# A two-block transformer on one core: eight-column norm sums, whole splits ahead of the residual, one norm for two, and a lone first weight block

## What is computed

```python
x = x + 0.5 * swiglu(rmsnorm(x, ffn1_norm_g), ffn1_w_in, ffn1_w_out)        # phase 0
x = x + merged @ w_mix_out                                                   # phase 1 (mix1)
x = x + 0.5 * swiglu(rmsnorm(x, ffn2_norm_g), ffn2_w_in, ffn2_w_out)        # phase 2
x = rmsnorm(x, final_norm_g)                                                 # phase 3 (final)
for i in range(2):          # phases 4, 5 (mix2), 6 and 7, 8 (mix3), 9
    h = modulate(rmsnorm_2(x, norm_g[i, 0]), sh1, sc1)     # h * (1 + scale) + shift
    x = x + 0.5 * g1 * swiglu_2(h, ffn_w13[i, 0], ffn_w2[i, 0])
    h = modulate(rmsnorm_2(x, norm_g[i, 1]), sh2, sc2)
    x = x + g2 * mixer(h)                                  # i == 0: pool and SSD; i == 1: attention
    h = modulate(rmsnorm_2(x, norm_g[i, 2]), sh3, sc3)
    x = x + 0.5 * g3 * swiglu_2(h, ffn_w13[i, 1], ffn_w2[i, 1])
return rmsnorm_2(x, final_norm_g_2)                                          # phase 10 (final)
```

## Time and profile before

| | before |
|---|---|
| median of 3 runs | 1699.43 us (1697.11 to 1700.32) |
| the profiled execution | 1698.5 us |
| its span, first to last instruction | 1696.7 us |
| PE busy | 1662.9 us (98%) |
| DVE busy | 1202.4 us (71%) |
| ACT busy | 809.9 us (48%) |
| mean granted PE clock | 0.996 |

### The profile page before, as it was taken

How to read it: one execution, slowest core, us unless ns; L and a number is a source line. 1 busy time by engine, 2 the same in 40 slices (tenths; PEclk the granted TensorE clock), 3 DMA queues, 4 the chain that set the end, 5 groups by cost and what they waited for, 6 DMA issues and landing times.

```text
span 1696.7 us, 34452 instructions
## 1 busy us (share of the span) xinstructions
PE 1662.9 (98%) x14542; PEld 1627.7 (96%) x14542; DVE 1202.4 (71%) x1303; ACT 809.9 (48%) x874; POOL 87.1 (5%) x110
## 2 busy tenths in 40 slices
PE   9999999999999999999998899999999999999998
PEld 9999999999999999999997899999999987899998
DVE  5888876676788887888867688756545566765444
ACT  5444456654544444444565553445444456554442
POOL 0000000000000000000004000000000003200000
PEclk9999999999999999999999999999999999999999
DMA  7988744344498875988533359653654443335551
GB/s 311 346 331 312 279 174 174 125 166 158 146 354 318 303 276 187 340 312 320 205 141 125 125 201 345 247 188 135 224 197 175 174 148 125 125 141 208 198 189 59
DMA packets 50491, 365.08 MB, mean 215 GB/s; under 512 B 5728, under 2 KB 5856, under 8 KB 6240
## 3 DMA queue, kind: packets, MB, share of 16 engines
q1 hardware_dynamic: 39744, 287.04, 46.0%
q0 software_dynamic: 10368, 75.50, 12.0%
q10 hardware_dynamic: 288, 1.18, 0.2%
HBM read 362.65 MB, written 1.05 MB: 214 GB/s over the span
## 4 chain that ended last, share of the span: by engine, by line
PE 88%; DVE 7%; ACT 3%; issue 1%; DMA 0%; SPq 0%; ACTq 0%; DVEq 0%
PE bank L252 50%; PE bank L284 24%; PE bank L267 3%; PE bank L244 3%; DVE wlo L184 2%; PE bank L357 2%; PE bank L1662 1%; PE bank L369 1%; DVE m_p L1427 0%; DVE m_e L1924 0%; ACT whi L176 0%; DVE x L309 0%; ACT m_e L1803 0%; DVE x L401 0%; PE bank L1231 0%
## 5 line engine op out<-in xcount | busy, mean ns | idle before, releaser
L184 DVE TENSOR_TENSOR wlo<-raw,whi 128x2048 fp32r<-128x2048 f32 x261 | 598.1, 2294 | 203.0 <-ACT whi L176 202.2
L252 PE MATMUL bank<-xh,whi 128*128 128x256 f32 x2608 | 728.0, 279 | 3.4 <-ACT gate L533 2.0
L252 PE MATMUL bank<-xl,whi 128*128 128x256 f32 x2608 | 723.3, 277 | 0.0
L252 PE MATMUL bank<-xh,wlo 128*128 128x256 f32 x2608 | 723.0, 277 | 0.0
L176 ACT ACTIVATE whi<-raw 128x2048 fp32r<-128x2048 f32 x261 | 498.4, 1913 | 312.5 <-PE bank L252 190.9
L252 PEld LDWEIGHTS bank<-xh,whi 128*128 128x128 f32 x2608 | 492.1, 189 | 6.1 <-issue 2.6
L252 PEld LDWEIGHTS bank<-xl,whi 128*128 128x128 f32 x2608 | 490.7, 188 | 0.1
L252 PEld LDWEIGHTS bank<-xh,wlo 128*128 128x128 f32 x2608 | 490.7, 188 | 0.0
L284 PE MATMUL bank<-hid_hi,whi 128*128 128x256 f32 x1056 | 292.8, 277 | 0.0
L284 PE MATMUL bank<-hid_lo,whi 128*128 128x256 f32 x1056 | 291.9, 276 | 0.0
L284 PE MATMUL bank<-hid_hi,wlo 128*128 128x256 f32 x1056 | 291.9, 276 | 0.0
(11 more groups left out here) (317 smaller groups left out, 1822.7 us busy)
## 6 DMA issues: line engine op xcount, KB each, us to landing
raw<-stream_in SPq DMA_DIRECT2D x270, 1024.0 KB, 4.8
mod_raw<-mod_in POOLq DMA_DIRECT2D x72, 1024.0 KB, 7.0
params<-params_in SPq DMA_DIRECT2D x1, 1474.0 KB, 16.1
x<-x_in SPq DMA_DIRECT2D x2, 512.0 KB, 4.3
m_gsu<-sgu_in ACTq DMA_DIRECT2D x1, 1024.0 KB, 5.1
y_out<-x SPq DMA_DIRECT2D x1, 1024.0 KB, 3.8
consts<-consts_in SPq DMA_DIRECT2D x1, 280.5 KB, 4.8
tab_pos<-pos_in ACTq DMA_DIRECT2D x1, 128.0 KB, 3.5
```

The costliest lines, as they stand in the source:

```text
L184: dve.tensor_tensor(wlo[:, s, :], raw[:, s, :], whi[:, s, :].bitcast(F32), ALU.subtract)\
L252: last = pe.matmul(out[:, m, :], (whi, wlo)[wp][:, s, k * 256 + m * P:k * 256 + m * P + P], (xh, xl)[ap][:, k, :], start=(k == 0 and j == ...
```

## The change

- **Norm sums (`pe_norm`, `act_norm`).** DVE's pair sums are gone, but for phase 0; PE sums each of the eight tiles, 16 matmuls of one column where there were eight. The dummy matmuls between the sums are gone; 8 stand behind the sums (before: 14) and 20 behind the spread (before: 26).
- **The second block of the next phase** is split whole, and ahead of the residual: on ACT where the halves were, on DVE before `mod_store` and the residual. In phase 0 the halves stay, both ahead of the reciprocal.
- **The final norm inside (phase 3).** Phase 3 has no program of its own left. At the norm of phase 4 ACT also squares `x * g_final` tile by tile, PE sums both kinds, and DVE and ACT make both reciprocal roots at once. `dve_final_inside` writes `x` normed by the final norm within phase 4, behind the last group of `mod_sum`; PE's `mod_fold` waits for it.
- **Shift in the rounding.** Mixers 2 and 3 take the shift as ACT's bias like the FFNs. `xm` stays without it, and its rows get two more columns that hold the shift, so that the float32 products have the shift's part in a column of their own, which ACT adds as a bias.
- **The start.** SP waits for `x` after the first weight block, and then issues the second and third. DVE's pair sums of phase 0 stand ahead of the constants' copies.
- `gres` (the residual's gain) and `gmod` (the next norm's) are now made behind `xl`.

```diff
+W = T + 2
...
-        xm = sb("xm", [P, KD, T])
+        xm_wide = sb("xm", [P, KD, W])
+        xm = xm_wide[:, :, 0:T]
...
+            ni = norm_index[n]
+            act.activation(std[:, 8:9], cols[:, 64:65], ACT.Sqrt)
             for b in range(4):
                 if n == 0:
                     act.wait_ge(sem(f"x_loaded{b // 2}"), 16)
                 else:
-                    act.wait_ge(sem("x_updated"), 4 * (n - 1) + b + 1)
+                    act.wait_ge(sem("x_updated"), 4 * last_stage(n) + b + 1)
                 act.activation(xm[:, 2 * b:2 * b + 2, :], x[:, 2 * b:2 * b + 2, :], ACT.Square, scale=D ** -0.5)\
                    .then_inc(sem("x_squared"), 1)
+                if n == AFTER_FINAL:
+                    for k in (2 * b, 2 * b + 1):
+                        act.activation(final_squares[:, k, :], x[:, k, :], ACT.Square, scale=prm("g_final")[:, k:k + 1])\
+                           .then_inc(sem("final_step"), 1)
...
+                act_split_halves(act)
+            if n == AFTER_FINAL:
+                act.wait_ge(sem("final_step"), KD + 2)
+                act.activation(std[:, 0:4], std[:, 0:4], ACT.Sqrt, scale=1.0 / D).then_inc(sem("std_ready"), 1)
+            else:
+                act.wait_ge(sem("x_summed"), ni + 1)
+                act.activation(std[:, 0:2], STAT[:, T:T + 2], ACT.Sqrt, bias=cols[:, 64:65]).then_inc(sem("std_ready"), 1)
...
-        WARM = (14, 8, 14, 26)
+        WARM = (8, 20)
...
+            def column_sums(squares, k, c0, first, last):
+                for tt in range(2):
+                    mm = pe.matmul(STAT[:, c0 + tt:c0 + tt + 1], squares[:, k, tt * P:tt * P + P], ones[:, 0:1],
+                                   start=(first and tt == 0), stop=last, skip_group_check=True)
+                return mm
...
             for b in range(4):
...
-                if b >= 2:
-                    pe_keep_warm(pe, n, WARM[b - 2])
-                pe.wait_ge(sem("x_paired"), 4 * n + b + 1)
-                for tt in range(2):
-                    mm = pe.matmul(STAT[:, T + tt:T + tt + 1], xm[:, 2 * b, tt * P:tt * P + P], ones[:, 0:1],
-                                   start=(b == 0 and tt == 0), stop=(b == 3), skip_group_check=True)
+                if n == 0:
+                    pe.wait_ge(sem("x_paired"), b + 1)
+                    mm = column_sums(xm, 2 * b, T, b == 0, b == 3)
+                    continue
+                pe.wait_ge(sem("x_squared"), 4 * ni + b + 1)
+                for k in (2 * b, 2 * b + 1):
+                    mm = column_sums(xm, k, T, k == 0, k == KD - 1)
+                if n == AFTER_FINAL:
+                    for k in (2 * b, 2 * b + 1):
+                        pe.wait_ge(sem("final_step"), k + 1)
+                        mm = column_sums(final_squares, k, T + 2, False, k == KD - 1)
             mm.then_inc(sem("x_summed"), 1)
-            pe_keep_warm(pe, n, WARM[2])
-            pe.wait_ge(sem("rstd_ready"), n + 1)
+            pe_keep_warm(pe, n, WARM[0])
+            pe.wait_ge(sem("rstd_ready"), ni + 1)
             for tt in range(2):
-                mm = pe.matmul(STAT[:, tt * P:tt * P + P], rstd[:, tt:tt + 1].to_broadcast([P, P]), ident,
+                c = tt + 2 if n == AFTER_FINAL else tt
+                mm = pe.matmul(STAT[:, tt * P:tt * P + P], rstd[:, c:c + 1].to_broadcast([P, P]), ident,
                                start=(tt == 0), stop=True, skip_group_check=True)
             mm.then_inc(sem("rstd_spread"), 1)
+            if n == AFTER_FINAL:
+                for tt in range(2):
+                    mm = pe.matmul(MODP[:, tt * P:tt * P + P], rstd[:, tt:tt + 1].to_broadcast([P, P]), ident,
+                                   start=(tt == 0), stop=True, skip_group_check=True)
+                mm.then_inc(sem("final_step"), 1)
             if phases[n][0] != "final":
-                pe_keep_warm(pe, n, WARM[3])
-            elif n + 1 < len(phases):
-                pe_keep_warm(pe, n, 60)
-
-        def dve_norm(dve, n, g, shift=None, split=True, whole=False):
-
-
+                pe_keep_warm(pe, n, WARM[1])
...
+        def dve_norm(dve, n, g, shift=None, split=True):
+
+            ni = norm_index[n]
             if n == 0:
-                for b in range(4):
-                    dve_pair(dve, n, b)
-            dve_split_half(dve, n, 0)
-            dve.wait_ge(sem("std_ready"), n + 1)
-            dve.reciprocal(rstd[:, 0:2], std[:, 0:2]).then_inc(sem("rstd_ready"), 1)
-            dve_split_half(dve, n, 1)
-            dve.wait_ge(sem("rstd_spread"), n + 1)
+                dve_split_halves(dve)
+            if n == AFTER_FINAL:
+                dve.wait_ge(sem("x_summed"), ni + 1)
+                dve.tensor_scalar(std[:, 0:2], STAT[:, T:T + 2], RMS_EPS, float(D), ALU.add, ALU.mult).then_inc(sem("final_step"), 1)
+                dve.wait_ge(sem("final_step"), KD + 1)
+                dve.scalar_tensor_tensor(out=std[:, 2:4], in0=std[:, 0:2], scalar=RMS_EPS, in1=STAT[:, T + 2:T + 4],
+                                         op0=ALU.mult, op1=ALU.add).then_inc(sem("final_step"), 1)
+            c = 4 if n == AFTER_FINAL else 2
+            dve.wait_ge(sem("std_ready"), ni + 1)
+            dve.reciprocal(rstd[:, 0:c], std[:, 0:c]).then_inc(sem("rstd_ready"), 1)
+            dve.wait_ge(sem("rstd_spread"), ni + 1)
             dst = xm if split else x
-            def add_shift(k):
-                dve.wait_ge(sem("xn_scaled"), 8 * shift_index[n] + k + 1)
-                dve.tensor_scalar(xm[:, k, :], xm[:, k, :], shift[:, k:k + 1], None, ALU.add).then_inc(sem("xn_ready"), 1)
             for k in range(KD):
                 ins = dve.scalar_tensor_tensor(out=dst[:, k, :], in0=x[:, k, :], scalar=g[:, k:k + 1],
                                                in1=STAT[:, 0:T], op0=ALU.mult, op1=ALU.mult)
...
-                elif whole:
-                    ins.then_inc(sem("xn_scaled"), 1)
-                    if k >= 1:
-                        add_shift(k - 1)
...
+                if split:
                     ins.then_inc(sem("xn_ready"), 1)
...
+            if not split:
+                return
+            if phases[n][0] in ("mix2", "mix3"):
+                dve.tensor_copy(xm_wide[:, :, T:W], shift.unsqueeze(2).to_broadcast([P, KD, 2])).then_inc(sem("shift_column"), 1)
+            for k in range(KD):
                 dve.wait_ge(sem("xn_rounded"), 8 * split_index[n] + k + 1)
-                if shift is None or whole:
+                if shift is None:
                     ins = dve.tensor_tensor(xl[:, k, :], xm[:, k, :], xh[:, k, :].bitcast(F32), ALU.subtract)
                 else:
                     ins = dve.scalar_tensor_tensor(out=xl[:, k, :], in0=xm[:, k, :], scalar=shift[:, k:k + 1],
                                                    in1=xh[:, k, :].bitcast(F32), op0=ALU.add, op1=ALU.subtract)
                 ins.then_inc(sem("xn_split"), 1)
...
+            if n in MOD_OF:
+                layer, j = MOD_OF[n]
+                dve.wait_ge(sem("x_updated"), 4 * (last_stage(n) + 1))
+                dve.tensor_scalar(gres[:, :], mod_col(layer, j + 2), 1.0 if j == 3 else 0.5, None,
+                                  ALU.mult).then_inc(sem("gres_ready"), 1)
+            dve_gain(dve, next_stage(n))
...
+        def dve_final_inside(dve):
+
+            g = prm("g_final")
+            dve.wait_ge(sem("final_step"), KD + 3)
+            for k in range(KD):
+                ins = dve.scalar_tensor_tensor(out=x[:, k, :], in0=x[:, k, :], scalar=g[:, k:k + 1], in1=MODP[:, 0:T],
+                                               op0=ALU.mult, op1=ALU.mult)
+                if k % 2 == 1:
+                    ins.then_inc(sem("x_updated"), 1)
...
+                if n == AFTER_FINAL:
+                    pe.wait_ge(sem("x_updated"), 4 * n)
...
             act_split(act, F0 + 33)
-            act_split_halves(act, n + 1)
+            act_split(act, F0 + 34)
...
+            if n == AFTER_FINAL:
+                dve_final_inside(dve)
...
             dve_split(dve, F0 + 33)
+            dve_split(dve, F0 + 34)
...
+                pe.wait_ge(sem("shift_column"), 1)
                 for k in range(KD):
-                    mm = pe.matmul(MODP[0:16, 0:T], prm("w_dt")[:, k * 16:k * 16 + 16], xm[:, k, :],
+                    mm = pe.matmul(MODP[0:16, 0:W], prm("w_dt")[:, k * 16:k * 16 + 16], xm_wide[:, k, :],
                                    start=(k == 0), stop=(k == KD - 1))
                 mm.then_inc(sem("m2_dt"), 1)
...
-                act.activation(r[0:16, 0, :], MODP[0:16, 0:T], ACT.Identity, bias=prm("dt_bias")[0:16, :])\
+                act.activation(cols[0:16, 67:68], MODP[0:16, T:T + 1], ACT.Identity, bias=prm("dt_bias")[0:16, :])\
+                   .then_inc(sem("shift_column"), 1)
+                act.wait_ge(sem("shift_column"), 2)
+                act.activation(r[0:16, 0, :], MODP[0:16, 0:T], ACT.Identity, bias=cols[0:16, 67:68])\
...
```

(6 more changed lines are left out.)

153 lines of the change are left out of this document (57 added, 96 removed).

## The result

| | before | after |
|---|---|---|
| median | 1698.33 us (4 runs) | 1715.53 us (4 runs, 1710.9 to 1719.56) |
| the profiled execution | 1698.5 us | 1710.9 us |
| its span | 1696.7 us | 1709.2 us |
| mean granted PE clock | 0.996 | 0.978 |

The ratio is 1.0095, with an interval of 1.0073 to 1.0117: slower, by about 1%. The prediction had 1694.1 us and a range of 1690 to 1708.

The account below looks back on a forecast made before the run. PE was taken to bound the kernel, holding 88% of the chain of waits. Terms -2.1 + 1.7 - 4.4 + 2.2 - 2.7 = -5.3 us took 1698.5 to 1693.2, with 0.9 for the median 1694.1 us; range 1690 to 1708.

Parts of the forecast that it names:

- likeliest case: Whole kernel: the terms' sum of -5.3 us comes in, 1694.1 us, own range 1690 to 1698; chance 0.58.
- Rival 1: PE at the norms: long one-column sums don't hold the granted clock, nearly every norm falls, 1707.7 us; chance 0.25.
- the norm sums with the whole split: Norms: 32 sums without pair sums, and the whole split ahead of the residual, cost +1.7 us; bounds 0 and +3.5.
- the final norm at the end of phase 4: DVE behind the last mod_sum: scalings and splits use up its cover and delay the residual, +2.2 us.
- start: Phase 0: first block lands 1 us sooner, so the second block begins 2.1 us earlier; bounds 0 and -3.5.
- merged norm: Phases 3 and 4: one norm of 15.5 us replaces 19.93 us, -4.4 us; bounds -5 and -3.
- shift in the rounding: Mixers 2 and 3: shift in ACT's bias saves 1.57 us each, together -2.7 us; bounds -3.1 and -1.5.
- Rival 2: DVE holds the late phases: final norm and splits cost upper bounds, mixer 2 and start gain nothing, 1699 us; chance 0.12.
- Rival 3: Pair sums' chain is not shortened, but all else comes in full: -9.4 us, 1690 us; chance 0.05.
- from -12 to +1: Whole kernel: span given for the summed change in us by the terms' bounds, said not to fall all together.
- the second block of phase 0: Start: the forecast would be wrong if this block started at 24 us or later.
- the granted clock of the windows behind the norms is below 1: PE behind the norms: a sign that would show the forecast wrong.

Follow-up runs that it names:

- wide64: The changed kernel with each column sum 64 columns wide instead of one: 1701.89 us, ratio 1.0025.
- halves: early with the split of the second block put back in halves, as in the kernel before: 1694.4 us, ratio 0.9974.
- one_halves: halves with column sums one column wide again: 1708.88 us, ratio 1.0059.
- shift_alone: The kernel before with only the shift added in the rounding, and two more columns in the dt and krope products: 1697.85 us, ratio 0.9984.
- pairs_halves: early with both the halved split and, but for the merged norm, the pair sums and dummies of the kernel before: 1690.12 us, ratio 0.9946.
- b_nodummy: The kernel before without dummies among the sums, and with 8 and 20 behind as in the changed kernel: 1697.7 us, ratio 0.9996.
- early: wide64 with the final norm moved from behind the five turns to the front of phase 4: 1696.9 us, ratio 0.9987.
- pairs: early with the pair sums and dummies of the kernel before in all norms but the merged one: 1710.01 us, ratio 1.0058.

## Why the prediction was wrong

The likeliest case was wrong, and its first rival, to which I gave 0.25, happened. Two steps failed. The forecast put nothing for the clock: it took 3.24 us of one-column sums to leave it up, and the runs show that it fell at all eight norms and the last, for some 13.6 us. And the forecast's own sum, -5.3 us, was too good by 7.8: the norm sums with the whole split, put at +1.7, cost 5.9, and the final norm at the end of phase 4, put at +2.2, cost 6.7. Rival 1 had corrected the first step and kept the second, so it had 1707.7 us where the kernel took 1715.5.

**The clock: the case was rated too low, and its price came out right in the sum alone.** I wrote that the longest stretch of nothing but column sums would grow from 0.95 to 3.24 us, and "What a long stretch of one-column matmuls does to the granted clock no row shows". I then took it that "PE is never idle within the sums" spoke against a fall. The two runs that differ in nothing but the width (wide64 and after; halves and one_halves) say 13.6 and 14.4 us for it by the medians (11.9 and 14.4 by the ratios); the rival had 8 x 1.7 = 13.6. That these agree is in part luck, since the spread over the norms was not the priced one: between wide64 and after the merged norm pays 5.9 us, phases 1, 2, 6 and 7 1.0 to 1.5, phases 8 and 9 2.3 and 2.6, and phase 5 nothing, since it had its fall in wide64 already. And of the same one-column sums in one_halves two norms, those of phases 8 and 9, paid nothing. By the section "What's actually happening" of "TensorE: Matmul & The Clock Gate" in the Trainium skill, the clock is gated by how busy PE has been. The trace agrees only if busy is not what the records show: in the merged norm they have PE busy for 2.00 of 2.00 us from 628 to 632 us at one column and at 64 alike, and only the latter kept the clock.

One row pointed this way. PE stayed at half rate in the start while it did sums and dummies by turns, which I named as speaking for the rival and then weighed at one in four. It was weak evidence, though: in shift_alone the same instructions stand there, and the clock came up sooner.

**What is left, 7.8 us, is in the forecast's own sum.** Without the clock (wide64) the kernel takes 1701.9 us, not 1694.1:

| step | forecast | measured | from |
|---|---|---|---|
| start | -2.1 | -1.2 (after), -2.1 (pairs_halves), -2.2 (b_nodummy) | second block of phase 0 |
| norm sums | with the split +1.7 | +4.1 | halves to pairs_halves: 3.5 in seven norms, 0.6 in the last |
| whole split | in the +1.7 | +1.8 | early to halves, seven norms |
| merged norm | -4.4 | -4.0 | wide64 |
| final norm at the end of phase 4 | +2.2 | +6.7 | wide64 to early, norm of phase 5 |
| shift in the rounding | -2.7 | -3.1 | shift_alone, norms of phases 5 and 8 |

- *Norm sums and split, +1.7.* This step failed in size: 5.9 together. I had 0.101 us for each sum, from a group of eight; 32 in a row took 3.70 us (0.11 each, and the root 3.74 behind the first, where I had 3.41). And I let each norm give back what the half splits and `gres` had cost DVE. In wide64 the scaling of phase 1 did start sooner, 1.27 us behind the root where before has 1.50, but the second block came 6.80 us behind the scaling instead of 6.61 and took nearly all of it back; why, I can't say.
- *Final norm, +2.2.* The mechanism was as told: DVE's cover used up, PE idle for 2.45 us where I had 2.4. What this term left out is the lower clock behind the idle, at which the 32 sums take 7.06 us instead of 3.76. That is 3.3 us of the missing 4.5.
- *Merged norm, -4.4; shift, -2.7.* Both within their bounds. ACT's squares did not hold the sums (root 7.8 us behind the first sum with the clock up, 7.2 in the forecast).
- *Start, -2.1.* The size was near, the reason was not. The block did not land sooner (ACT began at 9.93 us, 9.44 before; 9.31 in pairs_halves), and SP's order alone gave nothing. What pays is that the 14 and 8 dummies at half rate are gone from among the sums: the root starts 3.1 to 3.7 us behind the first sum instead of 5.77, and b_nodummy, which changes nothing but dummies, has all of the gain (22.43 us). A single profile of the start is a weak measure, though: shift_alone, with the start of before, has 22.85, by an earlier rise of the clock.

With the measured sizes the sum is -1.2 + 4.1 + 1.8 - 4.0 + 6.7 - 3.1 = +4.3 us without the clock's part; the medians of wide64 and before differ by 3.2 (1698.65 for before beside these runs), and the ratio 1.0025 is 4.2 us. Rival 2 had the right place (DVE at the end of phase 4) but not the clock in it. Rival 3 did not occur. One slip in the working: the lower end of "from -12 to +1" does not follow from the bounds as given. With the final norm, which had none, at its +2.2, they add up to -9.4 and +1.2. The chances don't rest on it.

Of what I said would show it, the second block of phase 0 at 23.37 us spoke for the forecast, and "the granted clock of the windows behind the norms is below 1" spoke against it in every norm behind the start.

**Where the expected gain is.** It was there, under the losses: pairs_halves keeps the start, the merged norm, the shift and the early final norm, and drops the two parts that cost. By the table its norms take 6.6 us less than before and its start 2.1, so 8.7; the medians differ by 8.4.

**What stays open.** The 1 to 5.6 us by which the stretches between the norms differ from profile to profile, with falls of the clock at changing places in phase 5 (between 926 and 943 us in before, 878 to 882 and 929 to 936 in pairs_halves), were not followed up. Why the clock falls at some norms and not at others of the same form (phase 8 of pairs, phases 8 and 9 of one_halves) is open too. Nor was it tried whether 32 columns would do.

## What to carry to other kernels

- A rise in PE's busy time with fewer instructions is a sign of its clock. Read the granted clock of 2 us windows at each place where the change leaves only narrow matmuls, and count such stretches as a risk even if PE is never idle in them. Here a sum over channels could be made 64 columns wide at no cost in time (3.76 us for 32 of them, 3.70 with one column), as a cheap insurance.
- A long instruction moved ahead of a residual or another hand-over to PE is paid by the gap that it opens, and by the clock behind that gap: the same whole split cost some 2 us with wide sums and 20 us where pair additions and dummies stood behind it.
- Dummy matmuls cost little where PE waits, and their full time where it doesn't; when a chain is shortened so that PE no longer waits, they must go, and what kept the clock has to be found elsewhere.
- Equal medians can hide a loss and a gain. Go through the stages of a run before you read "the same" as "it costs nothing": in b_nodummy the falls cost up to 0.9 us a norm, and the start gave 2.2 us back.

## What the runs showed of the hardware that I had not expected

- A matmul of one column and one of 64 columns, both float32, take the same time in a row of 32 (3.70 and 3.76 us in the norm of phase 1), yet PE's granted clock fell behind the first and not behind the second. With 16 columns it fell (0.50 in 202 to 204 us).
- The busy time in the records doesn't tell the difference: in the merged norm it is 2.00 of 2.00 us from 628 to 632 us in either.
- Removing the dummies among the sums from the kernel before lowered its mean granted clock from 0.996 to 0.988 and left its time as it was (0.9996, 0.9982 to 1.001). The falls cost 0.9 us at each of the norms of phases 1 and 2, and the start gained 2.2 us. The mean clock alone is thus no measure of what is lost.
- The same start took different times: the second block of phase 0 came at 24.61 us in before, 24.55 in start_alone and 22.85 in shift_alone, by when the clock came up.
